# Splitting the last four experts' down product by output columns in a two-block transformer kernel

## The reference, cut to what matters

```python
def expert_block(args):
    xb, e = args
    hdn = jax.nn.silu(xb @ w_gate[e]) * (xb @ w_up[e])      # 1024 -> 512
    return hdn @ w_down[e]                                  # 512 -> 1024
...
out = zeros.at[slot_tok].add(ys * slot_gate[:, None])
h = h + hier_moe(rmsnorm(h, ffn_norm[l]), ...)
return rmsnorm(h, final_norm)[:, N_META:]                   # sum of squares over all 1024 columns
...
x = layer_norm(alpha * x + 0.5 * swiglu(x, ffn_w_gate[l, 0], ffn_w_up[l, 0], ffn_w_down[l, 0]), ...)
```

## Time and profile before

| what | value |
|---|---|
| runs before | 2258.77, 2258.16, 2258.3 us; median 2258.3 us |
| the profiled execution | 2258.04 us, of which the traced span is 2256.0 us |
| busy in the span: PE, DVE, ACT | 1840.8, 859.8, 213.9 us |
| mean granted PE clock | 0.912 of full |
| chain that ended last | PE 63%, DMA 30%, DVE 3% |
| DMA in the expert stage | 426 to 428 GB/s in nearly every slice |

### The profile page before, as it was taken

The page is one execution under the profiler, slowest core; times in us unless marked ns, Lnnn a source line. Parts: engine busy times, 40 slices in busy tenths (PEclk is TensorE's granted clock), DMA queues, the critical chain, the costliest instruction groups (busy, mean ns, idle before and its releaser), DMA issues.

```text
span 2256.0 us, 26121 instructions
## 1 busy us (share of the span) xinstructions
PE 1840.8 (82%) x11348; PEld 1220.6 (54%) x11348; DVE 859.8 (38%) x1804; ACT 213.9 (9%) x407; POOL 17.9 (1%) x41
## 2 busy tenths in 40 slices
PE   8997556666656666565699999999999999989997
PEld 6764222222222222122299658699579946858973
DVE  2223111110111111110276742476776766347675
ACT  2320000000000000000110011000010002201000
POOL 1100000000000000000000000000000000000000
PEclk9998788888888887778899999999999999999999
DMA  9257999999999999999955543365545544315550
GB/s 277 96 227 289 427 428 427 428 428 427 428 426 428 428 427 428 428 428 428 376 179 167 190 150 130 113 205 177 179 148 170 187 149 149 112 56 187 178 187 27
DMA packets 183338, 604.62 MB, mean 268 GB/s; under 512 B 17773, under 2 KB 135975, under 8 KB 159159
## 3 DMA queue, kind: packets, MB, share of 16 engines
q1 hardware_dynamic: 177600, 595.51, 68.2%
q10 hardware_dynamic: 5623, 7.42, 1.0%
HBM read 601.86 MB, written 1.05 MB: 267 GB/s over the span
## 4 chain that ended last, share of the span: by engine, by line
PE 63%; DMA 30%; DVE 3%; SPq 3%; issue 1%; ACT 1%; ACTq 0%; DVEq 0%
PE banks L1257 24%; PE banks L1284 11%; DMA e_W<-in_expert_w_up 10%; DMA e_W<-in_expert_w_down 10%; DMA e_W<-in_expert_w_gate 9%; PE banks L889 6%; PE banks L1332 5%; PE banks L897 3%; PE banks L1376 3%; PE banks L1452 2%; PE banks L198 2%; SPq L143 1%; SPq L869 1%; DMA x_ring<-in_ffn_w_up 1%; PE banks L393 1%
## 5 line engine op out<-in xcount | busy, mean ns | idle before, releaser
L889 PE MATMUL banks<-e_W,e_xT 128*32 128x512 f32 x2048 | 288.8, 727 | 191.1 <-DMA e_W<-in_expert_w_up 103.4
L889 PEld LDWEIGHTS banks<-e_W,e_xT 128*32 128x32 f32 x2048 | 79.9, 131 | 387.8 <-issue 386.5
L897 PE MATMUL banks<-e_W,e_hT 128*32 128x512 f32 x960 | 136.8, 734 | 135.2 <-DMA e_W<-in_expert_w_down 135.2
L1257 PE MATMUL banks<-x_xs,x_sums 128*128 128x128 f32 x2112 | 243.0, 275 | 0.0
L1257 PEld LDWEIGHTS banks<-x_xs,x_sums 128*128 128x128 f32 x2112 | 239.4, 192 | 0.0
L1257 PE MATMUL banks<-x_xT,x_ring 128*128 128x128 f32 x1408 | 168.1, 279 | 8.5 <-DVE x_xT L1672 6.8
L1257 PEld LDWEIGHTS banks<-x_xT,x_ring 128*128 128x128 f32 x1408 | 164.0, 195 | 9.5 <-DVE x_xT L1672 7.5
L897 PEld LDWEIGHTS banks<-e_W,e_hT 128*32 128x32 f32 x960 | 37.9, 132 | 223.3 <-issue 223.3
L1059 DVE TENSOR_TENSOR c_h<-c_h,banks 128x1024 f32<-128x1024 f32 x32 | 39.1, 1221 | 305.2 <-PE banks L917 305.2
L1284 PE MATMUL banks<-x_sums,x_hs 128*128 128x512 f32 x264 | 125.0, 592 | 0.0
L1332 PE MATMUL banks<-x_xT,x_ring 128*128 128x256 f32 x544 | 121.6, 385 | 1.6 <-DVE x_xT L1672 1.6
(11 more groups left out here) (455 smaller groups left out, 2017.8 us busy)
## 6 DMA issues: line engine op xcount, KB each, us to landing
e_W<-in_expert_w_gate SPq DMA_DIRECT2D x64, 2048.0 KB, 20.9
e_W<-in_expert_w_up SPq DMA_DIRECT2D x64, 2048.0 KB, 20.6
e_W<-in_expert_w_down SPq DMA_DIRECT2D x64, 2048.0 KB, 21.5
x_ring<-in_ffn_w_gate SPq DMA_DIRECT2D x44, 1024.0 KB, 5.5
x_ring<-in_ffn_w_up SPq DMA_DIRECT2D x44, 1024.0 KB, 7.7
x_ring<-in_ffn_w_down SPq DMA_DIRECT2D x44, 1024.0 KB, 5.0
x_ring<-in_w_in_mlstm SPq DMA_DIRECT2D x13, 1024.0 KB, 5.2
x_ring<-in_w_in_conv SPq DMA_DIRECT2D x10, 1024.0 KB, 5.1
```

The source lines that it names most:

```text
L889: i = pe.matmul(ps[SLOT * j:SLOT * (j + 1), b, :], E.xT[:, x, k, SLOT * j:SLOT * (j + 1)], E.W[:, slot0 + j, k * DE:(k + 1) * DE], start=( ...
L897: i = pe.matmul(ps[SLOT * j:SLOT * (j + 1), 2 + c, :], E.hT[:, f, SLOT * j:SLOT * (j + 1)], E.W[:, slot0 + j, f * D + c * 512:f * D + (c + ...
L1257: mm = pe.matmul(ps[:, bank, lo + which * P:lo + (which + 1) * P], a, b, start=(k == 0), stop=(k == 3))
```

## The change

The last group's down chunks hold other parts of the matrices. Chunk 0 and 1 hold the left 512 output columns (hidden quarters 0 and 1, then 2 and 3), chunks 2 and 3 the right 512 columns. The bytes are the same; a row in a transfer is 2 KB long instead of 4 KB, and each chunk is issued as two DMAs of 1 MB instead of one of 2 MB. When the left half is complete, ACT copies it, PE combines it (two matmuls), DVE adds it, ACT squares and sums it; then the same for the right half. The left half's sum of squares is scaled by 1/1024, with eps added, in an instruction of its own (Identity) and becomes the bias of the root. Two semaphore sets of the mixers (`cs`, `ls`) are joined into one (`xs`) with higher counts; their waits are the same ones.

```diff
 def expert_chunk(K, c):
     if c >= XCHUNKS - QUAD:
-        return K.dram["expert_w_down"][0, QUAD * q:QUAD * (q + 1)].rearrange("e (p k) n -> p e k n", p=P)[:, :, j % QUAD, :]
+        return K.dram["expert_w_down"][0, QUAD * q:QUAD * (q + 1)].rearrange("e (p k) n -> p e k n", p=P)[:, :, 2 * (j % 2):2 * (j % 2) + 2, 512 * (j % QUAD // 2):512 * (j % QUAD // 2 + 1)]
...
             if c >= XCHUNKS - QUAD:
-                dst = dst.rearrange("p (e n) -> p e n", e=QUAD)
+                dst = dst.rearrange("p (e k n) -> p e k n", e=QUAD, k=2)
+                for k in range(2):
+                    sp.dma_start(dst[:, :, k, :], expert_chunk(K, c)[:, :, k, :]).then_inc(E.arrived[c % SLOTS], 16)
+                continue
...
+        def out_of_slice(c, m, f2):
+            pe.wait_ge(E.arrived[c % SLOTS], 16 * (c // SLOTS + 2))
+            w = E.W[:, c % SLOTS, :].rearrange("p (e k n) -> p e k n", e=QUAD, k=2)
+            for k in range(2):
+                for j in range(QUAD):
+                    i = pe.matmul(ps[SLOT * j:SLOT * (j + 1), 2 + m, :], E.hT[:, 2 * f2 + k, SLOT * j:SLOT * (j + 1)], w[:, j, k, :],
+                                  start=(f2 == 0 and k == 0), stop=(f2 == 1 and k == 1))
+            i.then_inc(self.spent, 1)
+
+        def combine_half(x, m):
+            for t in range(TT):
+                pe.matmul(ps[:, 6 - 2 * t + m, :], E.mixT[:, x, t, :], E.y[:, m * 512:(m + 1) * 512], start=True, stop=True)\
+                  .then_inc(self.c_mm, 1)
...
             else:
-                out_of_slices(at + 2 * QUAD)
+                pe.wait_ge(self.mix_out, QUADS)
+                for m in range(2):
+                    for f2 in range(2):
+                        out_of_slice(at + 2 * QUAD + 2 * m + f2, m, f2)
+                    pe.wait_ge(self.y_out, q + m + 1)
+                    combine_half(q % 2, m)
+                return
...
+    def last_tail(self, a):
+        K, E, N, ps = self.K, self.E, self.N, self.ps
+        for m in range(2):
+            cols = slice(m * 512, (m + 1) * 512)
+            a.wait_ge(self.spent, XCHUNKS - 2 + 2 * m)
+            a.activation(E.y[:, cols], ps[:, 2 + m, :], ACT.Copy).then_inc(self.y_out, 1)
+            for t in range(TT):
+                a.wait_ge(self.summed, TT * (QUADS - 1 + m) + t + 1)
+                K.ac(a, a.activation(N.junk[:, cols], K.h[:, t, cols], ACT.Square, accum_out=N.ss[:, m, t:t + 1]))
+                if m == 0:
+                    K.ac(a, a.activation(N.ss[:, 0, t:t + 1], N.ss[:, 0, t:t + 1], ACT.Identity, bias=K.eps[:, 0:1], scale=1.0 / D))
+                else:
+                    a.activation(N.root[:, t:t + 1], N.ss[:, 1, t:t + 1], ACT.Sqrt, bias=N.ss[:, 0, t:t + 1], scale=1.0 / D)\
+                     .then_inc(self.sumsq, 1)
...
             if q == QUADS - 1:
                 early_sums()
+                for m in range(2):
+                    cols = slice(m * 512, (m + 1) * 512)
+                    for t in range(TT):
+                        v.wait_ge(self.c_mm, TT * (q + m) + t + 1)
+                        v.tensor_tensor(K.h[:, t, cols], K.h[:, t, cols], ps[:, 6 - 2 * t + m, :], ALU.add).then_inc(self.summed, 1)
+                return
...
-            for t in range(TT):
-                a.wait_ge(moe.summed, TT * (QUADS - 1) + t + 1)
-                K.ac(a, a.activation(N.junk[:, :], h[:, t, :], ACT.Square, accum_out=N.ss[:, t:t + 1]))
-                a.activation(N.root[:, t:t + 1], N.ss[:, t:t + 1], ACT.Sqrt, bias=K.eps[:, 0:1], scale=1.0 / D).then_inc(s["sumsq"], 1)
```

More of the change, by code:

```diff
@@ L1022, in scalar @@
                 a.activation(N.warm[:, :], K.eps[:, 3:4], ACT.Sqrt)
+            if q == QUADS - 1:
+                return self.last_tail(a)
             a.wait_ge(self.spent, at + 3 * QUAD)
@@ L1147, in whole @@
     nc, ps, sem, dram, h = K.nc, K.ps, K.sem, K.dram, K.h
-    names = ("spent", "used", "sum", "post", "hsum", "tx", "lone", "kept", "act", "hid", "bank", "mv", "root", "zn", "turned", "xt_v", "xt_a", "rows", "sumsq", "stored",
+    names = ("spent", "used", "sum", "post", "hsum", "tx", "lone", "kept", "act", "hid", "bank", "mv", "root", "zn", "turned", "xt_v", "xt_a", "rows", "stored",
              "ld_lstm")
@@ L1151, in whole @@
     arrived = [sem(f"s_arrived{n}") for n in range(RING)]
[L1152 to L1155, removed]
+    xs = {n: sem("x_" + n) for n in ("qx", "xs_mm", "xmax", "xp", "xt_mm", "xt_out", "xo_mm", "xo_out", "xy_mm", "xy_out")}
+    cs = {n: sem("c_" + n) for n in ("gate", "pad", "b")}
+    ls = {n: sem("l_" + n) for n in ("gates", "na", "lf", "em_in", "em", "row", "pad", "conv", "silu", "va", "og", "bc_mm", "col_mm",
                                      "col", "wt", "masked", "sc_mm", "pt", "num_mm", "hv", "hroot", "ogg", "y", "y_mm", "y_out")}
@@ L1341, in scores, with turn_p @@
                                    K.memk[:, layer, hh, :], start=True, stop=True)
-                mm.then_inc(a["xs_mm"], 1)
-            def turn_p(a):
-                pe.wait_ge(a["xp"], TT * XH)
+                mm.then_inc(xs["xs_mm"], 1)
+            def turn_p(layer):
+                pe.wait_ge(xs["xp"], TT * XH * (layer + 1))
                 for n in range(TT * XH):
@@ L1349, in turn_p, with attend @@
                                          X.xp[:, n, m * P:(m + 1) * P], K.ident[:, :])
-                i.then_inc(a["xt_mm"], 1)
-            def attend(a, layer):
-                pe.wait_ge(a["xt_out"], 1)
+                i.then_inc(xs["xt_mm"], 1)
+            def attend(layer):
+                pe.wait_ge(xs["xt_out"], layer + 1)
                 for n in range(TT * XH):
@@ L1358, in attend, with turn_o @@
                                        start=(m == 0), stop=(m == 1))
-                mm.then_inc(a["xo_mm"], 1)
-            def turn_o(a):
-                pe.wait_ge(a["xo_out"], 1)
+                mm.then_inc(xs["xo_mm"], 1)
+            def turn_o(layer):
+                pe.wait_ge(xs["xo_out"], layer + 1)
                 for m in range(2):
@@ L1390, in conv @@
                 group(at + 2, 2)
-                scores(cs, 0)
+                scores(0)
                 group(at + 3, 3)
                 group(at + 4, 0)
-                turn_p(cs)
+                turn_p(0)
                 pe.wait_ge(cs["gate"], 1)
@@ L1573, in ffn, with exps, p_out @@
                 norm(j + 1)
-            def exps(q):
-                a.wait_ge(q["xmax"], 1)
+            def exps(layer):
+                a.wait_ge(xs["xmax"], layer + 1)
                 for n in range(TT * XH):
                     a.activation(X.xp[:, n, :], ps[:, 4 + n // 2, (n % 2) * NM:(n % 2 + 1) * NM], ACT.Exp, bias=X.xmx[:, n:n + 1],
-                                 scale=SC, accum_out=X.xsum[:, n:n + 1]).then_inc(q["xp"], 1)
-            def p_out(q):
-                a.wait_ge(q["xt_mm"], 1)
+                                 scale=SC, accum_out=X.xsum[:, n:n + 1]).then_inc(xs["xp"], 1)
+            def p_out(layer):
+                a.wait_ge(xs["xt_mm"], layer + 1)
                 a.activation(X.xpT[:, :, :, :].rearrange("p n m t -> p (n m t)"), ps[:, 4:8, :].rearrange("p b n -> p (b n)"),
-                             ACT.Copy).then_inc(q["xt_out"], 1)
+                             ACT.Copy).then_inc(xs["xt_out"], 1)
             def conv():
@@ L1592, in conv @@
                 gate(0)
-                exps(cs)
+                exps(0)
                 gate(1)
-                p_out(cs)
+                p_out(0)
                 gate(2)
@@ L1606, in lstm @@
                 a.activation(X.em[:, :], X.em[:, :], ACT.Exp, scale=-1.0).then_inc(ls["em"], 1)
-                exps(ls)
-                p_out(ls)
+                exps(1)
+                p_out(1)
                 for g in range(6):
@@ L1893, in conv @@
                 product(0)
-                highest(cs)
+                highest(0)
                 product(1)
                 product(2)
-                attended(cs)
+                attended(0)
                 gated(0)
-                turned_out(cs)
+                turned_out(0)
                 gated(1)
@@ L2073, in network @@
         N, E, M, X, Y = Kit(), Kit(), Kit(), Kit(), Kit()
-        at = place(nc, N, "n_", at, end, lnT=f(P, 170), stats=f(P, TT, 2, 6), mv=f(P, TT, 2), root=f(P, TT), ss=f(P, TT), warm=f(P, 1))
+        at = place(nc, N, "n_", at, end, lnT=f(P, 170), stats=f(P, TT, 2, 6), mv=f(P, TT, 2), root=f(P, TT), ss=f(P, 2, TT), warm=f(P, 1))
         at = place(nc, K, "k_", at, end, gate=f(P, 2, TT), slot=f(P, 2, TT), slotq=f(P, QUADS, 2 * TT),
```

61 lines of the change are left out of this document (31 added, 30 removed).

## The result

| | before | changed kernel |
|---|---|---|
| median of 8 runs each | 2258.42 us | 2264.74 us |
| range of the runs | 2257.82 to 2259.54 | 2263.71 to 2265.77 |
| the profiled execution, its span | 2258.04, 2256.0 | 2264.92, 2263.2 |

The ratio is 1.0027, with a 95% interval of 1.0018 to 1.0037: the change costs 4.1 to 8.4 us.

The account below looks back on a forecast made before the run. It took the second ring chunk, DVE's early sums, then PE without a gap as the bound. 2258.04 + 5.1 (order on ACT) + 0.8 (2 KB rows) = 2263.9, plus 0.3 to the median: 2264.2 us, range 2260.8 to 2267.5.

Parts of the forecast that it names:

- The bound at the seam: Before PE's first feed-forward matmul at 1121.78: the second ring chunk and DVE's early sums bound; nothing later gives time back.
- The order on ACT: At the last tail: right copy queued behind left squares that wait for early sums, putting the right half in series; +5.1 us.
- T: End of DVE's early sums, 1115.52 before; PE's first feed-forward matmul was T + 6.26, forecast T + 11.4.
- The clock in the combination: PE's right combination, two matmuls: half clock after idling, 3.8 us; at full clock 2.02 us.
- Rows of 2 KB: Last four down chunks: shorter rows make the ring chunks land later, +0.8 us, bounds -0.8 and +2.4.
- the +8 us that the prediction weighed for four more DMAs: Last down chunks' transfers: four more DMAs at a fixed 2 us each, giving 2272; the trace was said not to agree.
- The cover of those issues: On SP: four more down issues cost nothing, beginning over 15 us before the first landing; uncovered, about 0.4 us each.
- The clock at the feed-forward's start: PE's first 32 feed-forward records, 5.47 us before: no difference taken; bounds about -1.8 and +1.9.
- A: Rival at the seam: not slower, early sums end before the last down chunk lands; -2.5 us, 2255.8; chance 0.06.
- B: Rival, within 0.2%: ACT's order as forecast, PE combines at full clock, 2 KB rows free; +3.5, 2261.8; chance 0.12.
- C: Rival, slower still: 2 KB rows at 1 KB rows' pace, first feed-forward block wholly at half clock; 2267.7; chance 0.16.
- D: Rival after the seam: delay given back later, or the semaphores' count makes something else; 2258.3; chance 0.04.

## Why the prediction was right, and where its terms were off

The forecast was 2264.2 us, with 2260.8 to 2267.5; measured were 2264.7. The mechanism was the one that was named; that the number came within half a microsecond is in part luck, as the sum below shows.

- **The bound at the seam.** It was put on the second ring chunk and early sums, and on nothing behind 1121.78 giving anything back. The move of early sums shows it for the changed kernel: 10.6 us between the medians. For the kernel before, the run with two DMAs for each chunk shows it: PE was done sooner and nothing moved. Without early sums on the way the kernel before gained 1.6 us by its median and perhaps nothing, as the wait of only 0.19 us for PE had said: there two bounds lay side by side.
- **The order on ACT, +5.1 us.** Measured 4.87 in the profile: T + 11.1 for T + 11.4. The signs named for it are there: the right copy 2.87 us after the left addition (1116.80 to 1119.67; 2.8 was named), PE idle for 9.91 us (9), DVE waiting 4.36 us between left and right additions (4). Turning round either order took 3.5 and 5.6 us away. A copy whose data lay ready at 1110.4 stood until 1119.67 behind squares without data. The Trainium skill (*TensorE: Matmul & The Clock Gate*, "Architectural detail: the array is 16× 32×32, not 1× 128×128") has the queues of ACT and DVE as strictly first in, first out; the trace agrees.
- **The clock in the combination.** Half was taken, 3.8 us to the last result; it was 3.67, at half clock for all but the end. Kept busy, PE needed 1.98 (2.0 was put down).
- **Rows of 2 KB, +0.8 us.** The sign was right and the size too small: 1.2 us (27.17 against 26.01 from the start of the last up products, means of six profiles and of two), inside the bounds of -0.8 and +2.4. The term took the cost of a row from chunks of 4 KB and 1 KB rows; the value lies nearer to the pace of 1 KB rows than a cost per row makes it. That it is the rows and not the eight issues, the run with two DMAs for each chunk shows; with it the +8 us that the prediction weighed for four more DMAs is gone too. The cover of those issues was thinner than I said: SP was busy with them until 1097.08, and with the right copy first its next issue came at 1097.36, more than a microsecond after the hidden product at 1096.01. It cost nothing that a run shows: the second ring chunk still landed 5.6 to 5.9 us behind the last down chunk, with SP held up or not.
- **The clock at the feed-forward's start, 0.** This was the term that was missed: 6.68 against 5.47 us, +1.2 in the profile, within the bound of +1.9. The reason given, a like pattern of work and gaps before, was too weak: over the kernels the block took 3.84 to 6.68 us. How much of the 1.2 is the change's is open. With two DMAs and the order of before the block took 6.35 us, and there is one profile of each kernel.
- **The sum.** +5.1 + 0.8 was named; the profiles have 4.87 + 1.36 + 1.21 = 7.4 at the mixed products, 7.2 in the span and 6.9 in the times of the two profiled executions (2258.04 and 2264.92). The medians differ by 6.3. So rows and clock were put 1.8 us too low together, the order 0.2 too high, and 1.1 us of the difference in the profiles is not in the medians; that these nearly cancel is luck. Of T's 1.36 us, 0.2 belongs to that scatter: PE started on the last up products 0.16 us later in the changed kernel's profile.
- **The rivals.** A would have needed early sums to end before the last down chunk; they ended 6.5 us after its product. B fell with the clock, at half in the combination, and with the rows, which did cost something. C came half true: the ring chunks landed 1.2 us later, not 2.4, and the first block took 6.68 us, of some 7.4 wholly at half clock. D fell with the span: of 7.44 us lost at the mixed products 7.2 were left at the end. What A described is what a better kernel makes of the change: with early sums out of the way half the tail does hide.

## What to carry to other kernels

Splitting a step so that its first half runs early paid here only once every engine that the first half passes through could take it early. Where one of them had an unrelated wait ahead of it (DVE's sums of the next stage's weights), the first half became a plug in ACT's order for the second. Before splitting, write down for each engine the order of its instructions with the time at which each has its data, and put no instruction ahead of one whose data is there sooner. An engine that does filler work for a later stage should do it behind the critical tail, in a gap that the trace shows, and not ahead of it.

## What was not expected of the hardware

- A gap on PE cost twice here: the wait itself, and the clock behind it. 8.85 us of useless matmuls in the gap made the changed kernel 2.9 us faster, because the 1.98 us of combination and the 3.84 us of the first block then ran at full clock.
- Where the gap before the last down product was 0.89 us, the product took 1.92 us; where it was 3.40 us, with the same data and the same instructions, it took 3.64 to 3.69. Over the ten profiles, with 16 records each, it took 1.92 us behind gaps of 0.89 to 2.33 us and 2.60 to 3.64 us behind gaps of 3.18 to 3.40.
- Issuing a DMA can hold SP for long. Eight issues of 1 MB took 14.42 us with rows of 4 KB and 19.96 with rows of 2 KB. In the kernel before, the third ring chunk's issue took 10.12 us, where the first took 0.37. It showed in no landing that these kernels wait for at the seam.
